# GpSimd instead of VectorE for the low parts of sixteen weight halves in a three-block transformer kernel

## The reference, cut to what matters

```python
x = first_block(...)      # attention with an index, pooling, and a mixture of 32 experts
for layer in range(2):    # second_block
    h = rmsnorm_2(x, norm_gains[layer])
    if layer % 2 == 0:    # "recurrence" block: even_layer
        z = h @ w_in      # split: lru_x, lru_gate, q, k, v, swa_gate
        lru_x = causal_depthwise_conv(lru_x, conv_w, conv_b)
        y_a = rg_lru(lru_x, ...) * silu(lru_gate)
        y_b = sliding_window_gqa_sinks(q, k, v, sinks) * silu(swa_gate)
        x = x + concatenate([y_a, y_b]) @ w_out
    else:                 # third block: odd_layer
        z = h @ w_in      # split: c_q, c_kv, k_rope, mla_gate, dq, dk, dv, diff_gate
        y_c = causal_mla_attention(...) * silu(mla_gate)
        y_d = norm(causal_diff_attention(...)) * silu(diff_gate)
        x = x + concatenate([y_c, y_d]) @ w_out
```

## Time and profile before

| what | value |
|---|---|
| median of 3 executions | 2349.46 us (2347.33 to 2351.78) |
| the profiled execution, its own time | 2358.7 us |
| its span, first to last instruction | 2356.9 us |
| mean granted TensorE clock | 0.976 |
| TensorE matmul busy | 2089.4 us (89%), 14538 instructions |
| VectorE busy | 1252.0 us (53%), 2281 instructions |
| ScalarE busy | 858.9 us (36%), 1312 instructions |
| GpSimd busy | 55.2 us (2%), 56 instructions |
| share of the last chain: TensorE, DMA, VectorE, ScalarE | 49%, 34%, 8%, 4% |

### The profile page before, as it was taken

How to read it: one execution, slowest core, us unless ns; L and a number is a source line. 1 busy time by engine, 2 the same in 40 slices (tenths; PEclk the granted TensorE clock), 3 DMA queues, 4 the chain that set the end, 5 groups by cost and what they waited for, 6 DMA issues and landing times.

```text
span 2356.9 us, 38440 instructions
## 1 busy us (share of the span) xinstructions
PE 2089.4 (89%) x14538; PEld 1364.2 (58%) x14538; DVE 1252.0 (53%) x2281; ACT 858.9 (36%) x1312; POOL 55.2 (2%) x56
## 2 busy tenths in 40 slices
PE   6899998989988888888888888999999999997997
PEld 2677766762222222222222222998889999997887
DVE  3455567545444444444444445558866454577655
ACT  3333344431111111111111113457855444565543
POOL 0000000000000000000000001011100010010000
PEclk9999999999999999999999999999999999998998
DMA  9998987899999999999999999463445455542442
GB/s 368 354 348 291 310 285 233 299 350 364 427 428 428 428 427 427 427 428 428 428 427 427 427 428 372 166 208 121 134 152 182 153 177 182 175 147 88 135 134 91
DMA packets 135047, 695.43 MB, mean 295 GB/s; under 512 B 14992, under 2 KB 15120, under 8 KB 85264
## 3 DMA queue, kind: packets, MB, share of 16 engines
q1 hardware_dynamic: 134928, 693.79, 76.7%
HBM read 691.63 MB, written 2.10 MB: 294 GB/s over the span
## 4 chain that ended last, share of the span: by engine, by line
PE 49%; DMA 34%; DVE 8%; ACT 4%; SPq 3%; issue 2%; DVEq 0%; ACTq 0%
PE acc L1185 34%; DMA ring<-in_w 30%; DMA land<-in_stream_a 3%; PE psO L1237 3%; PE psS L1468 3%; PE acc L1182 3%; DVE WL L1945 2%; SPq L1043 2%; ACT WH L1636 1%; DMA land<-in_stream_bc 1%; PE psM L1454 1%; PE acc L1454 1%; PE psT L1119 1%; ACT SB L1722 0%; PE psO L1127 0%
## 5 line engine op out<-in xcount | busy, mean ns | idle before, releaser
L1185 PE MATMUL acc<-HH,WH 128*128 128x256 f32 x2152 | 633.8, 295 | 11.8 <-DVE HL L1969 5.4
L1945 DVE TENSOR_TENSOR WL<-land,WH 128x1024 fp32r<-128x1024 f32 (+2 forms) x346 | 417.4, 1208 | 417.7 <-ACT WH L1636 413.6
L1185 PE MATMUL acc<-HH,WL 128*128 128x256 f32 x2152 | 616.0, 286 | 0.0
L1185 PE MATMUL acc<-HL,WH 128*128 128x256 f32 x2152 | 615.2, 286 | 0.0
L1636 ACT ACTIVATE WH<-land 128x1024 fp32r<-128x1024 f32 (+2 forms) x350 | 362.4, 1037 | 222.3 <-PE acc L1185 176.8
L1185 PEld LDWEIGHTS acc<-HH,WH 128*128 128x128 f32 x2152 | 420.5, 195 | 34.6 <-issue 11.6
L1185 PEld LDWEIGHTS acc<-HH,WL 128*128 128x128 f32 x2152 | 420.6, 195 | 2.0 <-issue 1.0
L1185 PEld LDWEIGHTS acc<-HL,WH 128*128 128x128 f32 x2152 | 419.9, 195 | 0.0
L1468 PE MATMUL psS<-ring,low 128*32 128x512 f32 x2048 | 273.9, 607 | 105.3 <-DMA ring<-in_w 100.8
L1468 PEld LDWEIGHTS psS<-ring,low 128*32 128x32 f32 x2048 | 40.8, 108 | 316.4 <-DMA ring<-in_w 285.0
L2355 DVE TENSOR_TENSOR X<-acc,X 128x512 f32<-128x512 f32 x128 | 88.6, 692 | 218.9 <-PE acc L1454 218.9
(11 more groups left out here) (370 smaller groups left out, 2413.4 us busy)
## 6 DMA issues: line engine op xcount, KB each, us to landing
ring<-in_w SPq DMA_DIRECT2D x384, 1024.0 KB, 26.0
land<-in_stream_a SPq DMA_DIRECT2D x284, 512.0 KB, 7.6
land<-in_stream_bc SPq DMA_DIRECT2D x246, 512.0 KB, 4.0
land<-in_stream_bc SPq DMA_DIRECT2D x12, 384.0 KB, 3.5
X<-in_xT SPq DMA_DIRECT2D x1, 2048.0 KB, 14.0
out<-low SPq DMA_DIRECT2D x4, 512.0 KB, 2.6
cst<-in_const SPq DMA_DIRECT2D x1, 1514.5 KB, 9.6
low<-in_w_pool SPq DMA_DIRECT2D x1, 1024.0 KB, 8.3
```

Of the source, the lines that this page charges most:

```text
L1185: mm = pe.matmul(bank[:, 0:S], w[:, kk, :], h[rows[kk]], start=(z == 0 and i == 0), stop=stop)
L1945: ins = dve.tensor_tensor(wl, src, wh, ALU.subtract)
```

## The change

The engine of a `lo` step is no longer the argument of `load` alone. `load` keeps the argument as a default, and picks GpSimd for the second half (h = 1) of the units lx and lg with an even number and of dg and mg with an odd number: four units of each name, sixteen halves. Their high parts, landing slots and TensorE steps are the same; GpSimd's list gets the sixteen steps at the places where VectorE's list had them.

```diff
-    def load(self, n=1, by="dve"):
+    def load(self, n=1, by0="dve"):
 
         for key, h in self.ahead[:n]:
             q = len(self.halves)
+            by = "pool" if h and (key[0] in ("lx", "lg") and key[1] % 2 == 0 or key[0] in ("dg", "mg") and key[1] % 2) else by0
             self.halves.append([])
@@
-    o.load(4, by="pool")
+    o.load(4, by0="pool")
```

## The result

The changed kernel takes 2351.31 us and the kernel before 2347.22 us (medians of 22 runs each, taken together). The ratio is 1.0021 with a 95% interval of 1.0013 to 1.0028: slower, by about 4.9 us (0.0021 x 2347). The forecast was 2352.2 us on an older median of 2349.46, that is +2.8 us. The sign is right and the size a little over half. That the changed kernel's median, 2351.31, lies within 0.9 us of the forecast is luck: the kernel before came out 2.2 us lower than the median that the forecast started from.

The account below looks back on a forecast made before the run. TensorE was taken to be all but full, with VectorE the fullest helper. Relief 0, lg 6 hold 1.06 and lower clock 1.7 gave +2.8 us on 2349.46, so 2352.2 us; 8-in-10 range 2345.5 to 2357.0.

Parts of the forecast that it names:

- Gain 0 from the removed work: TensorE's waits in the recurrence: none hangs on a removed VectorE low part, so 19.9 us less VectorE work gains 0.
- Third block and lx 0: 0 each: Eight low parts of dg and mg, and lx 0: VectorE idle time there covers the blocking, 0 each.
- Five others: 0: lx 2, lx 4, lx 6, lg 2, lg 4: VectorE held 1 to 2.4 us, delay ends in idle time; taken as 0.
- lg 6: 1.06 us: Softmax head's small two-input instruction held by GpSimd's low part, so exponents, gate copies and TensorE come 1.06 us later.
- the extra 1.3 us: At lg 6, if one-input work were held too, VectorE's 1.33 us would also come later: sum 1.3 us more.
- The clock: 1.7 us, behind lg 6: TensorE's gate copy wait grows from 1.35 to 2.41 us, and a lower clock after it costs 1.7 us.
- lg 0: "I take 0 and keep 2.4 for the range": Low part ready amid four scalings TensorE waits for; GpSimd assumed to let the burst end, 0, otherwise up to 2.4 us.
- a sign of being wrong (4 us or more): TensorE's wait before the first transposes at 4 us or more would mean the scaling was blocked.
- GpSimd gets into the scaling: Rival at lg 0: GpSimd interrupts the burst, 2.4 us of wait and 1.7 of clock more, 2356.4 us; chance 0.18.
- Its clock price: In the rival of a blocked scaling at lg 0: lower clock for about twice as long, 1.7 us more.

Follow-up runs that it names:

- experiment 4: Changed kernel, but GpSimd makes only 8 of 1024 columns of each of the sixteen low parts, the rest left out; ratio to before 1.0006.
- experiment 3: Kernel before with only the eight low parts of dg and mg on GpSimd; ratio to before 1.0006.
- experiment 10: Changed kernel with the low parts of lg 0 and lg 6 back on VectorE, fourteen on GpSimd; ratio to before 0.9989.
- experiment 1: Changed kernel with the low part of lg 0 back on VectorE, fifteen on GpSimd; ratio to before 1.0019.
- experiment 5: Changed kernel, with GpSimd's low part of lg 0 waiting for the VectorE scaling that TensorE's transposes wait for; ratio to before 1.0017.
- experiment 9: Kernel before with only the low part of lg 6 on GpSimd; ratio to before 0.9998.
- experiment 2: Kernel before with only the low part of lg 0 on GpSimd; ratio to before 1.0021.
- experiment 6: Changed kernel, with GpSimd's low parts of lg 0 and lg 6 waiting for VectorE's scaling and last softmax head of the recurrence; ratio to before 1.0002.
- experiment 8: Changed kernel with waits for lg 0 and lg 6, and one scaling moved earlier in VectorE's list; ratio to before 1.0014.
- experiment 11: Kernel before, VectorE's order changed: five scalings, last attention output and two mixed low parts ahead of weight low parts; 2344.92 us, ratio 0.9979.
- experiment 12: Kernel before with VectorE's scalings, last attention output and two mixed low parts earlier, plus the sixteen low parts on GpSimd; 2347.93 us, ratio 0.9996.

## Why the prediction was right or wrong

Point by point:

- *Gain 0 from the removed work.* Right, and shown by experiment 4: with GpSimd's instructions cut short the relief is worth nothing (168.47 against 168.44 us). The reason was read from the earlier trace rows: the pair of low parts ahead of the scaling belongs to a unit that is not moved.
- *Third block and lx 0: 0 each.* Right by experiment 3 and, beside the clock, by the distance from lg 7 to mg 7; for lx 0 by experiment 10. *Five others: 0.* Right by experiment 10, which has them on GpSimd.
- *lg 6: 1.06 us.* Right in place, kind and nearly in size: 0.91 us (2.26 - 1.35), and the same with lg 6 alone. The blocked instruction is the one named, of four elements, and the one-input reduction ahead of it was not held (1.22 us), so the extra 1.3 us that the prediction names for that case do not appear.
- *The clock: 1.7 us, behind lg 6.* In the changed kernel the granted clock is 0.57 in the stretch from 1694 to 1698, so it did fall there, and from lg 5 to lg 6 1.46 us more go by than before. It fell there in experiments 1 and 5 too, each losing 1.6 us more to the clock up to lg 7 than before. But in experiment 9 the same wait of 2.25 us is followed by six microseconds at 1.00. So this term is there in some executions or variants and not in others, and it is open what decides.
- *lg 0: "I take 0 and keep 2.4 for the range".* This is the step that failed. The prediction held that a burst of four instructions with no waits in it would keep GpSimd out. It did not: GpSimd came in after 0.73 us and TensorE's first wait became 4.50 us, which the prediction itself names as a sign of being wrong (4 us or more). The rule that it quotes for this rival held without waits in between as well. That is the rival "GpSimd gets into the scaling", with 2.15 us for the 2.4 foreseen. Its clock price was too high: the lower clock covers 6.8 us from 1629.3 instead of 3.4, but begins while TensorE still waits, so at lg 0 there are 2.70 us lost in experiment 2, 0.55 more than the wait, not 1.7.

The sum with the step put right is 0.9 + 2.15 of waits, 0.55 and 1.46 of clock, and 0.57 back for the small wait that TensorE no longer meets: 4.5 us, against 4.42 in the trace and 4.9 (3.1 to 6.6) in time. The chance given to that rival was 0.18; a row that showed a ready GpSimd instruction beside such a burst would have been worth more than the argument. The nearest one was at hand: the pair of low parts at 1681.47 in the earlier trace rows, which the prediction itself reads as GpSimd coming in between the two, has no idle time in it either. All terms of the mended sum are read from these traces, so that it comes out shows only that no large term is missing. The forecast's own total of 2.8 us is near the truth in part by luck: it has all of the loss at lg 6, where the trace of experiment 1 has 1.83 us, and nothing at lg 0, where that of experiment 2 has 2.70.

What stays open is how the two places add up in the median. Lg 0 alone costs 1.0021 and everything but lg 0 1.0019, each as much as both together (1.0021). In the distances to lg 7 they add (2.70 + 1.83 = 4.53 for 4.42). Behind lg 7 the lower clock takes a different share in each trace: 3.4 us are lost to it in experiments 3, 4, 6 and 9, 5.1 in experiment 10, 5.0 to 5.1 in experiments 1, 2 and 5, and 6.8 in the changed kernel, but also 6.8 in the profiled execution of the kernel before, which was slower (2358.7 us) than any of its 22 timed ones. So some of the loss may lie behind lg 7, as more time at the lower clock. One execution of each kernel cannot settle that, and the intervals of some 3 us leave room for it.

## What to carry to other kernels

Work given to GpSimd is not out of VectorE's way: here each moved subtraction of 1.24 us takes a port for 2.4 us, and what counts is which VectorE instruction is due in that window, not how full VectorE is. Look at the instructions at the moment when the GpSimd one becomes ready; where one is on the path, let GpSimd wait for it (experiment 6: one wait more at each of the two places, and the loss is gone). Such a wait is tied to the order of the list: when the order changed (experiment 8), the same two waits no longer helped. And before moving work between engines, see whether the late step can simply stand earlier in its own engine's list: this gave 0.2% (experiment 11, 0.03% to 0.39%) where the move cost 0.2%.

## What the runs showed of the hardware

- GpSimd takes the shared port also between instructions of VectorE that have no wait between them: a burst of four one-input scalings (128x256, SBUF to SBUF) took 3.48 us for 1.32, in the changed kernel and with lg 0 alone. One-input scalings are held elsewhere too: the eight of the convolution take 1.00 us in the mean after the change and 0.47 before, and 0.47 again in experiment 4, where GpSimd's instructions are short:

```profile
L2285 DVE TENSOR_SCALAR low<-low,col 128x256 f32<-128x256 f32 x8 | 8.0, 1004 | 1.0 <-POOL low L2422 0.7
```

```profile
L2284 DVE TENSOR_SCALAR low<-low,col 128x256 f32<-128x256 f32 x8 | 3.8, 471 | 0.3
```

- What was held beside a GpSimd subtraction and what was not: a two-input instruction of four elements was (0.94 us for 0.16), a scan of 128x256 was (2.72 us for 0.69), a reduction was not (1.22 us), nor was a reciprocal of 128x512. VectorE's low part, the reciprocal behind it and GpSimd's low part beside both, in the third block after the change:

```profile
2120.65 3.24 POOL L2414 TENSOR_TENSOR WL<-land,WH 128x1024 fp32r<-128x1024 f32 x1 [0.33 <-ACT WH L1637]
...
2120.41 1.23 DVE L1946 TENSOR_TENSOR WL<-land,WH 128x1024 fp32r<-128x1024 f32 x1
2122.56 3.35 DVE L2322 RECIPROCAL high_bc<-high_bc 128x512 f32<-128x512 f32 x1 [0.92 <-ACT high_bc L1761]
```

  GpSimd's takes 3.24 us for 2.4; it begins 0.99 us before VectorE's of 1.23 ends; the reciprocal's 3.35 is what it took before the change.
- A wait of TensorE of 2.25 us was followed by a stretch at the lower clock in some kernels (all sixteen, experiments 1, 5 and 12) and not in another (experiment 9). With lg 6 alone the clock is full behind it; with fifteen low parts on GpSimd, behind a wait of 2.3 us, it is 0.72. Columns as in the stretches above:

```profile
1698.00:1704.00 6.00, 5.43 (x47) 5.22 (x45) 5.13 (x12) 5.81 (x9) 1.34 (x1) 1.00 0.45 136
```

```profile
1696.00:1702.00 6.00, 5.89 (x36) 5.89 (x37) 5.00 (x10) 5.84 (x8) 1.34 (x1) 0.72 0.38 107
```
